# A two-block transformer on one core: round 2 of each feed-forward stage laid out anew, constants multiplied in TensorE's first waits, the first weight piece's rest moved to GpSimd, attention's roundings moved to the end of their slot

## The reference

```python
def swiglu(x, w_in, w_out):
    gate, up = jnp.split(x @ w_in, 2, axis=-1)
    return (jax.nn.silu(gate) * up) @ w_out
...
for l in range(DEPTH):
    mod = cond @ ada_w[l] + ada_b[l]
    shift, scale, gate = jnp.split(mod, 3, axis=-1)
    h = rms_norm(x, norm_g[l]) * (1.0 + scale[:, None, :]) + shift[:, None, :]
...
for i in range(DEPTH):
    h = layer_norm(DN_ALPHA * h + 0.5 * swiglu(h, ffn_w_in[i, 0], ffn_w_out[i, 0]), ln_g[i, 0], ln_b[i, 0])
    ...
    h = layer_norm(DN_ALPHA * h + m, ln_g[i, 1], ln_b[i, 1])
    h = layer_norm(DN_ALPHA * h + 0.5 * swiglu(h, ffn_w_in[i, 1], ffn_w_out[i, 1]), ln_g[i, 2], ln_b[i, 2])
```

## Time and profile before

| | |
|---|---|
| median of 3 runs | 2767.73 us (2767.6 to 2770.81) |
| profiled execution, own time | 2771.28 us |
| its span, first to last instruction | 2769.8 us |
| TensorE busy | 2661.6 us, 96% |
| VectorE busy | 1942.5 us, 70% |
| ScalarE busy | 1068.2 us, 39% |
| GpSimd busy | 574.2 us, 21% |
| granted TensorE clock, mean | 0.987 |

### The profile page before, as it was taken

One profiled execution on the slowest core, in us unless ns is written; L12 is line 12 of the kernel. 1 busy time (PEld: TensorE's weight loads), 2 busy tenths in 40 slices (PEclk: granted clock), 3 DMA queues, 4 the chain that ended last, 5 costly groups with the idle time before them and its releaser, 6 DMA issues.

```text
span 2769.8 us, 38462 instructions
## 1 busy us (share of the span) xinstructions
PE 2661.6 (96%) x15907; PEld 2312.8 (83%) x15907; DVE 1942.5 (70%) x2631; ACT 1068.2 (39%) x1518; POOL 574.2 (21%) x366
## 2 busy tenths in 40 slices
PE   5999999999999999999999999999999999989998
PEld 5777877678899998888899988999978778779997
DVE  5888744456788875548888788888744643888887
ACT  3434555552433434343333333343322222343332
POOL 1112000011344400001444214443000000044430
PEclk9999999999999999999999999999999999999999
DMA  7444221112233332222333323333323223223331
GB/s 263 140 145 132 77 61 61 61 62 76 92 103 111 92 107 77 92 61 63 106 107 97 117 77 102 112 92 107 126 83 107 73 68 103 61 92 107 92 122 46
DMA packets 289857, 268.32 MB, mean 97 GB/s; under 512 B 10567, under 2 KB 256593, under 8 KB 288401
## 3 DMA queue, kind: packets, MB, share of 16 engines
q1 hardware_dynamic: 286448, 256.98, 30.0%
q0 software_dynamic: 2368, 6.64, 0.7%
q10 hardware_dynamic: 864, 2.23, 0.2%
HBM read 263.72 MB, written 2.10 MB: 96 GB/s over the span
## 4 chain that ended last, share of the span: by engine, by line
PE 77%; DVE 15%; ACT 4%; issue 2%; DMA 1%; POOL 1%; SPq 0%; DVEq 0%; ACTq 0%; POOLq 0%
PE psum L351 13%; PE psum L353 13%; PE psum L352 13%; PE psum L429 7%; PE psum L430 6%; PE psum L431 6%; PE psum L408 2%; PE psum L407 2%; PE psum L406 2%; DVE w_lo L336 2%; DVE acc L525 1%; PE psum L3176 1%; DVE stat L674 1%; PE psum L2720 1%; DVE acc L684 1%
## 5 line engine op out<-in xcount | busy, mean ns | idle before, releaser
L351 PE MATMUL psum<-h_hi,w_hi 128*128 128x256 f32 (+1 forms) x2288 | 741.8, 324 | 27.8 <-DVE w_lo L1046 15.4
L353 PE MATMUL psum<-h_hi,w_lo 128*128 128x256 f32 (+1 forms) x2288 | 724.0, 316 | 0.0
L352 PE MATMUL psum<-h_lo,w_hi 128*128 128x256 f32 (+1 forms) x2288 | 723.5, 316 | 0.0
L351 PEld LDWEIGHTS psum<-h_hi,w_hi 128*128 128x128 f32 x2288 | 442.2, 193 | 61.2 <-issue 17.5
L352 PEld LDWEIGHTS psum<-h_lo,w_hi 128*128 128x128 f32 x2288 | 442.4, 193 | 28.5 <-issue 4.8
L353 PEld LDWEIGHTS psum<-h_hi,w_lo 128*128 128x128 f32 x2288 | 441.6, 193 | 27.0
L982 POOL TENSOR_TENSOR val<-w_raw 128x512 f32<-128x512 f32 x72 | 105.8, 1470 | 1285.1 <-DMA w_raw<-in_ffn_w_in 990.1
L336 DVE TENSOR_TENSOR w_lo<-w_raw,w_hi 128x2048 fp32r<-128x2048 f32 x102 | 234.5, 2311 | 146.6 <-ACT w_hi L331 137.8
L525 DVE SCALAR_TENSOR_TENSOR acc<-psum,acc 128x512 f32<-128x512 f32 x416 | 270.5, 680 | 47.6 <-PE psum L431 47.6
L351 PE MATMUL psum<-t_hiffn,w_hi 128*128 128x256 f32 x864 | 247.0, 286 | 2.5 <-DVE f_cffn L1063 2.5
L331 ACT ACTIVATE w_hi<-w_raw 128x2048 fp32r<-128x2048 f32 x104 | 197.2, 1911 | 134.2 <-PE psum L431 69.0
(11 more groups left out here) (429 smaller groups left out, 5396.0 us busy)
## 6 DMA issues: line engine op xcount, KB each, us to landing
w_raw<-in_ffn_w_in SPq DMA_DIRECT2D x176, 512.0 KB, 5.1
w_raw<-in_ffn_w_out SPq DMA_DIRECT2D x88, 512.0 KB, 6.4
w_raw<-in_ret_w_in SPq DMA_DIRECT2D x48, 512.0 KB, 4.7
ada_raw<-in_ada_w SPq DMA_DIRECT2D x32, 512.0 KB, 4.6
w_raw<-in_odd_w_in SPq DMA_DIRECT2D x32, 512.0 KB, 4.9
w_raw<-in_even_w_in SPq DMA_DIRECT2D x24, 512.0 KB, 7.4
w_raw<-in_gla_w_in SPq DMA_DIRECT2D x24, 512.0 KB, 4.8
ada_first<-in_ada_w SPq DMA_DIRECT2D x8, 1024.0 KB, 9.5
```

What stands on the lines that cost most here:

```text
L351: k.nc.tensor.matmul(out, ws, xs, start=first, stop=False)
L352: k.nc.tensor.matmul(out, ws, xl, start=False, stop=False)
L353: return k.nc.tensor.matmul(out, wl, xs, start=False, stop=last)
```

## The change

Five places are edited.

1. Way into the seven products: in `scalar_ffn` and `vector_ffn` the units of piece a of round 2 are rounded during round 1's last steps, T1's rounding goes behind them, and round 2 gets an order of its own (`vector_seventh`) in which A1 of piece b goes ahead of S, and piece o of round 1 is made in halves. TensorE waits for `w_s` separately (at P1), SyncE for `w_s` too before it overwrites that buffer. GpSimd loads the norm rows one sum set later.
2. The start: `tensor_warm` multiplies constants and the first tile of x into a bank that nobody reads, 5, 2 and 3 times.
3. The two parts of `lower` leave the gaps between the first row blocks and go behind them.
4. The first piece's rest is made by GpSimd in four parts (`gpsimd_first`), for which TensorE waits part by part.
5. In attention the piece at point 1 of a slot is rounded at the slot's end, and some additions to `acc` go ahead of a maximum or a piece.

```diff
@@ sync_piece
-    if n >= SLOTS:
+    if n == SLOTS:
+        k.nc.sync.wait_ge(*k.at("pool_w", ("rest", 3)))
+    elif n > SLOTS:
         k.nc.sync.wait_ge(*k.at("w_lo", n - SLOTS))
+        if PIECES[n - SLOTS][1:] == ("b", SEVEN):
+            k.nc.sync.wait_ge(*k.at("w_s", n - SLOTS))
@@ tensor_seven
+        if x == 1 and r == SEVEN:
+            pe.wait_ge(*k.at("w_s", n))
@@ scalar_ffn
+    n = AT[stage, "a", SEVEN]
+    scalar_unit_a22(k, n)
     scalar_hidden_split(k, stage, 1, 0)
     scalar_hidden(k, stage, 1, 1)
+    scalar_unit_s(k, n)
     scalar_hidden_split(k, stage, 1, 1)
+    scalar_unit_a1(k, n)
     scalar_t(k, stage, "T1")
-    n = AT[stage, "a", SEVEN]
-    scalar_unit_a22(k, n)
-    scalar_unit_s(k, n)
-    scalar_unit_a1(k, n)
...
         scalar_first(k, stage, r, 0)
+        scalar_unit_a1(k, AT[stage, "b", r])
         if r == SEVEN:
+            scalar_piece(k, AT[stage, "o", r - 1])
             scalar_unit_s(k, n)
-            scalar_piece(k, AT[stage, "o", r - 1])
-        scalar_unit_a1(k, AT[stage, "b", r])
+            scalar_products(k, stage, r, 0)
+            scalar_first(k, stage, r, 1)
+            scalar_hidden_split(k, stage, r, 0)
+            n = AT[stage, "a", r + 1]
+            scalar_unit_a22(k, n)
+            scalar_products(k, stage, r, 1)
+            scalar_unit_s(k, n)
+            scalar_hidden_split(k, stage, r, 1)
+            scalar_unit_a1(k, n)
...
@@ new, called by vector_ffn for round 2
+def vector_seventh(k, stage):
+    r = SEVEN
+    n, n_o = AT[stage, "b", r], AT[stage, "o", r - 1]
+    vector_unit_a22(k, n)
+    vector_mid(k, stage, r, 0, 0)
+    vector_mid(k, stage, r, 0, 1)
+    vector_unit_a1(k, n)
+    vector_mid(k, stage, r, 0, 2)
+    vector_piece_half(k, n_o, 0)
+    vector_c11(k, stage, r, 0)
+    vector_unit_s(k, n, 0)
+    vector_c12(k, stage, r, 0)
+    vector_unit_s(k, n, 1)
+    vector_products(k, stage, r, 0)
+    k.nc.vector.wait_ge(*k.at("f_h", (stage, r, 0)))
+    vector_mid(k, stage, r, 1, 0)
+    vector_hidden_split(k, stage, r, 0)
+    vector_mid(k, stage, r, 1, 1)
+    vector_piece_half(k, n_o, 1)
+    vector_mid(k, stage, r, 1, 2)
+    n = AT[stage, "a", r + 1]
+    vector_unit_a22(k, n)
+    vector_c11(k, stage, r, 1)
+    vector_c12(k, stage, r, 1)
+    vector_products(k, stage, r, 1)
+    vector_unit_s(k, n, 0)
+    vector_unit_s(k, n, 1)
+    vector_hidden_split(k, stage, r, 1)
...
@@ the start
+def gpsimd_first(k):
+    po, n = k.nc.gpsimd, AT["even", "qf", 0]
+    po.wait_ge(*k.at("w_hi", n))
+    for c in range(4):
+        x = slice(c * T, (c + 1) * T)
+        po.tensor_tensor(k.lo(n)[:, x], k.w_raw[:, buffer(n), x], k.hi(n)[:, x].bitcast(F32), SUB
+                         ).then_inc(*k.up("pool_w", ("rest", c)))
+WARM = (5, 2, 3)
+def tensor_warm(k, n):
+    for _ in range(n):
+        k.nc.tensor.matmul(k.bank[6][:], k.ident, k.acc[:, 0, 0:T], start=True, stop=True)
@@ attention
-    {-2: ("odd", "out", 1), 1: ("odd", "out", 2)}, {-2: ("odd", "out", 3), 1: ("ffn00", "a", 0)})]
+    {-2: ("odd", "out", 1), 1: ("odd", "out", 2)}, {-1: ("odd", "out", 3), 1: ("ffn00", "a", 0)})]
         scalar_turned(k, p, 3)
+        scalar_slot_piece(k, p, 1)
         scalar_slot_piece(k, p, 2)
...
+        if p == 4:
+            vector_outs(k, p, 3)
         vector_max(k, p, 3)
-        vector_outs(k, p, 3)
+        if p != 4:
+            vector_outs(k, p, 3)
         vector_filled(k, p, 0, fill)
         vector_scale(k, p, 3)
+        vector_outs(k, p, 4)
         vector_slot_piece(k, p, -1)
-        vector_outs(k, p, 4)
...
     vector_gated(k, 7)
     vector_gated_rest(k, 7)
+    vector_slot_piece(k, 7, 1)
```

More of the change, by code:

```diff
@@ L325, in scalar_piece @@
     if gated(n):
-        k.nc.scalar.wait_ge(*k.at("gated_even" if PIECES[n][0] == "even" else "gated", n))
+        k.nc.scalar.wait_ge(*k.at("gated_even" if PIECES[n][0] == "even" else "pool_w", n))
     else:
@@ L378, in half_step, with project_half @@
                  kk == 0, kk == KD - 1)
-def project_half(k, S, n, half, banks, steps=range(KD)):
+def project_half(k, S, n, half, banks, steps=range(KD), rests=None):
     for kk in steps:
+        if rests and kk % 2 == 0:
+            k.nc.tensor.wait_ge(*k.at(rests, ("rest", kk // 2)))
         if kk % 2 == 0:
@@ L1191, in vector_hidden_split @@
     vector_split(k, s, k.f_h[:, s, :], (stage, r, s), *ffn_oh(k, stage, r))
+def vector_seventh(k, stage):
[26 more added lines that the diff above has]
+    vector_hidden_split(k, stage, r, 1)
+    vector_outs_ffn(k, stage, r - 1, range(2))
+    vector_unit_a1(k, n)
+    vector_outs_ffn(k, stage, r - 1, range(2, 4))
+    n = AT[stage, "b", r + 1]
+    vector_unit_a22(k, n)
+    vector_unit_s(k, n, 0)
+    vector_outs_ffn(k, stage, r - 1, range(4, 6))
+    vector_unit_s(k, n, 1)
+    vector_outs_ffn(k, stage, r - 1, range(6, 8))
 def vector_ffn(k, stage):
@@ L1214, in vector_ffn @@
     vector_hidden(k, stage, 1, 0)
+    n = AT[stage, "a", SEVEN]
+    vector_unit_a22(k, n)
     vector_hidden_split(k, stage, 1, 0)
     vector_hidden(k, stage, 1, 1)
+    vector_outs_ffn(k, stage, 0, range(2))
+    vector_unit_s(k, n, 0)
+    vector_outs_ffn(k, stage, 0, range(2, 3))
     vector_hidden_split(k, stage, 1, 1)
[L1218 to L1223, removed]
+    vector_outs_ffn(k, stage, 0, range(3, 4))
     vector_unit_s(k, n, 1)
     vector_unit_a1(k, n)
+    vector_t_rest(k, stage, "T1")
     vector_outs_ffn(k, stage, 0, range(4, 8))
-    n = AT[stage, "b", SEVEN]
-    vector_unit_a22(k, n)
-    for r in range(SEVEN, ROUNDS):
+    vector_seventh(k, stage)
+    for r in range(SEVEN + 1, ROUNDS):
         last = r == ROUNDS - 1
         vector_mid(k, stage, r, 0, 0)
-        if r > SEVEN:
-            vector_piece(k, AT[stage, "o", r - 1])
+        vector_piece(k, AT[stage, "o", r - 1])
         vector_mid(k, stage, r, 0, 1)
-        if r == SEVEN:
-            vector_unit_s(k, n, 0)
         vector_mid(k, stage, r, 0, 2)
-        if r == SEVEN:
-            vector_unit_s(k, n, 1)
-            vector_piece(k, AT[stage, "o", r - 1])
         vector_unit_a1(k, AT[stage, "b", r])
@@ L1412, in scalar_start @@
     sc.activation(k.vcol[:], k.bank[0][:, 0:P], ACT.Copy).then_inc(*k.up("vcol", 0))
+    scalar_piece(k, AT["even", "qf", 0])
     sc.wait_ge(*k.at("lb_max", 0))
     sc.activation(k.lbt[:], k.lbt[:], ACT.Exp).then_inc(*k.up("lb_exp", 0))
-    scalar_piece(k, AT["even", "qf", 0])
     sc.wait_ge(*k.at("col8", "even"))
@@ L1465, in vector_start @@
         vector_modulated_tile(k, "even", t)
-    vector_first(k, 3)
-    ve.wait_ge(*k.at("vcol", 0))
-    vector_lower(k)
-    vector_first(k, 4)
-    vector_lower_sum(k)
-    for n in range(5, KD - 1):
+    for n in range(3, KD - 1):
         vector_first(k, n)
@@ L1474, in vector_start @@
     vector_first(k, KD - 1, 1, 2)
-    vector_piece(k, AT["even", "qf", 0])
+    ve.wait_ge(*k.at("vcol", 0))
+    vector_lower(k)
     mod = k.mod[:, 0, 0:16]
@@ L1681, in tensor_even @@
         bk = [flip(i, b) for b in range(8)]
-        pe.wait_ge(*k.at("w_lo", n_qf))
         if i == 0:
             pe.wait_ge(*k.at("mod", (0, "scale")))
-            project_half(k, S, n_qf, 0, (bk[0], bk[1]))
+            project_half(k, S, n_qf, 0, (bk[0], bk[1]), rests="pool_w")
             tensor_turn_tile(k, S, 2, STREAM[S])
@@ L1698, in tensor_even @@
         else:
+            pe.wait_ge(*k.at("w_lo", n_qf))
             pe.wait_ge(*k.at("e_u", i - 1))
@@ L2030, in gpsimd_program @@
     gpsimd_start(k)
+    gpsimd_first(k)
     gpsimd_even(k)
```

25 lines of the change are left out of this document (19 added, 6 removed).

## The result

| | before | changed |
|---|---|---|
| median, 5 runs each | 2767.73 us | 2739.3 us (2738.66 to 2740.87) |
| ratio, 95% interval | | 0.9896 (0.9884 to 0.9907) |
| profiled execution, own time | 2771.28 us | 2738.66 us |
| its span | 2769.8 us | 2737.2 us |

The forecast was 2736.4 us, a gain of 31.3. The medians are 28.4 apart, the two profiled spans 32.6.

What follows compares the result with a forecast made beforehand. TensorE, busy 96%, bounds the kernel, so only its waits or a faster clock can save time. Ways in 20.8, start 5.0 and attention 5.5 sum to 31.3 us: from the 2767.73 median to 2736.4 us, range 2722 to 2751 (own range 2729 to 2743).

Steps and rivals of the forecast that it cites:

- The pause and the clock behind it: Way into each feed-forward stage: waits of 26.7/4 us plus 2.35 us of slow clock, 9.0 us wasted per stage.
- What is late next: Rounds 2 and 3: S of piece b late by 0.5 us at P1; then waits of 1.9 at P4, 1.1 at P5.
- the heavier rival: Rounds 2 and 3: sums of 8 us and more, long pause in round 3, clock falls; 1.8 per stage, 2750 us; chance 0.26.
- Sums beside VectorE: GpSimd's four sums for piece b of round 3 take 7.2 us beside VectorE's work, instead of 5.6 us undisturbed.
- The sum of the stages: Ways into the four feed-forward stages: 9.0 + 0.3 less 1.1 and 3.0, 5.2 us each, 20.8 us in all.
- The start: Kernel start: first product's 48 matmuls end at 45.2, a gain of 5.8, taken as 5.0 us; bounds 1.2 and 6.5.
- GpSimd's four parts: Start, 35.1 to 40.5: run beside VectorE's rests of the features and may make the first 0.5 to 1 us late.
- five multiplications: Start: constants multiplied from 19.4, three slow at 1.8 us and two fast at 0.9, ending at 26.3.
- the first seven multiplications: Start: five before the turning, so it runs at full clock in 3.8 us, and two more after it, to 31.7.
- the 48 matmuls of the first products: Start: after three last constant multiplications they run at full clock in 5.8 us instead of 8.4.
- Attention: Waits in slots 0, 2, 4 and 7 shortened by reordering: sum stated as 6.0, taken as 5.5 us; bounds 3.5 and 6.3.
- Its four terms: Attention: 1.67 us each in slots 0 and 2, some 1.0 in slot 4, 1.33 in slot 7.

Runs made afterwards that it cites:

- the gate in parts: Changed kernel with GpSimd's multiplication of a piece by the gate in four 128x512 instructions in place of one of 128x2048: ratio 0.9886.
- the last kernel: Changed kernel with first piece and gate in parts, two last constant multiplications, S earlier, two additions to acc between products and split: 2724.54 us, ratio 0.9841.

## Why the prediction held, step by step

- **The pause and the clock behind it** (9.0 us a stage wasted): right. The 3.9 us wait and the stretch at 0.80 went in all four stages. That the wait itself lets the clock fall is borne out by moving A1 alone: the wait went, and with it the slow stretch in three stages of four. The 2.35 us of clock per stage were those of one execution; others with the same wait lose less in some stages.
- **What is late next**: right in place and size. P1 of the second half waits 0.55 us (0.5 forecast), P4 of round 3 1.64 (1.9), P5 0.85 (1.1). The cause given, that `w_s` of round 3's piece a stands behind the products, is shown: with S earlier both waits vanish. The forecast also reckoned with no loss of clock at these waits, since they are short. That held in the changed kernel, but the fall behind the 1.73 us wait in ffn10, with A1 moved alone, shows that the heavier rival was nearer than its text says.
- **Sums beside VectorE**: right. GpSimd's four sums for piece b of round 3 ran from 731.08 to 738.20, 7.1 us, where I took 7.2. The full lock of the two engines' port that the Trainium skill states ("SBUF — State Buffer", section "SBUF: two separate sides") shows plainly in attention (4.85 us in place of 0.48). In the ways in, though, it cost no more than the forecast. That this is because the sums are short instructions, between which VectorE gets its turn, is argued; what the gate in parts shows in attention fits it.
- **The sum of the stages**: 20.8 forecast; 21.8 by matched starts, about 20.2 against the mean of three executions with the old ways in, and 20.2 with that place alone.
- **The start**: the term that was too large, 5.0 against 3.1 to 3.5. Two steps of it failed. "GpSimd's four parts ... may make the first 0.5 to 1 late" was 1.9 (1.4 of it at the columns behind `mod`, of which I had not thought), so the first product came at 41.1 and not at 39.4. Part of this is a slip in the sum: five multiplications, three at 1.8 and two at 0.9, end at 26.6 by its own prices, not at 26.3; they ended at 27.19, and the one-column sums at 35.95 instead of 35.3. And the first seven multiplications, with the turning at full clock, won nothing, as the row blocks end at 32.6 or earlier either way; only the last three count. That the sums come earlier is the work of the turning's earlier start and of the row blocks without gaps. That the 48 matmuls of the first products would run in 5.8 us at full clock was right. The half-clock stretch and these products in the changed kernel, beside the earlier trace rows:

```profile
35.87:39.28 3.41, 3.41 (x5) 1.39 (x5) 2.88 (x5) 1.31 (x3) 3.41 (x4) 0.50 0.97 381
41.13:46.95 5.82, 5.82 (x48) 5.82 (x49) 4.77 (x9) 3.84 (x6) 0.00 (x0) 1.00 1.08 368
```

- **Attention**: 5.0 against 5.5. Its four terms (1.67, 1.67, 1.0 and 1.33) add up to 5.7, not to the 6.0 that it states. The slots gave 1.8, 1.8, 1.3 and 1.5. Of these 6.4, 1.1 were lost again at the wait for the probabilities and 0.3 before it. The 1.1 is a step that the prediction lacked: earlier work of VectorE now meets GpSimd's long multiplication by the gate. The trace of the kernel before had such a meeting to see, in a place where TensorE did not wait for it; the same pair takes 0.48 us in its other six places:

```profile
576.63 4.65 DVE L2330 TENSOR_SCALAR o_P<-o_P,o_l 128x128 f32<-128x128 f32 x2
```

- **The last 3 us**: the forecast took a gain worked out from one profiled execution off the median. That execution stood 3.5 us above its median, and the changed kernel's 0.6 below its own, which is the whole difference between the spans (32.6) and the medians (28.4). Much of it is chance in where the clock is at half: 2 us at the start and about 1.6 on the ways in. With 20.2 for the ways in, 3.3 for the start and 5.0 for attention the parts add up to 28.5. Against the forecast of 31.3 that is 1.7 less at the start, 0.6 less on the ways in and 0.5 less in attention. The interval of the ratio is 3.2 us either way, so the agreement of 28.5 with the medians is no proof of these parts.

## What to carry to other kernels

When the worst wait of a chain goes, follow the lists of all engines on to the next one: here each removed wait let a smaller one appear (3.9, then 1.6 at P4, then 1.55 at an output), and three more orders were tried until none of these was left. A piece of work that moves to GpSimd is not free for VectorE: cut it into short instructions, and look at what VectorE does in that time, above all tiny operations on the critical path. Short instructions shorten the delay and don't remove it: at the start GpSimd's work was in four parts, and two operations on 128x8 still took 1.71 us instead of 0.34. An operation that is put ahead of others in order to free something must have its own input by then: read the time at which that is ready before moving it.

## What the runs showed that was not expected

- An operation of VectorE on 128x2 elements takes 2.99 us, and two on 128x128 take 4.85, where GpSimd works on 128x2048; with four instructions of 128x512 in its place the longest takes 1.09. The four take 5.14 us in all instead of 4.58.
- A wait costs TensorE more than its idle time. Matmuls of 256 columns start 0.12 us apart; around the wait at P5 in the changed kernel they stand so:

```profile
746.61 0.28 PE L356 MATMUL psum<-h_lo,w_hi 128*128 128x256 f32 x1
746.73 0.28 PE L357 MATMUL psum<-h_hi,w_lo 128*128 128x256 f32 x1
747.86 0.38 PE L355 MATMUL psum<-h_hi,w_hi 128*128 128x256 f32 x1 [0.85 <-DVE consts L1068]
748.08 0.28 PE L356 MATMUL psum<-h_lo,w_hi 128*128 128x256 f32 x1
748.20 0.28 PE L357 MATMUL psum<-h_hi,w_lo 128*128 128x256 f32 x1
```

From 746.73 to 748.08 are 1.35 us where 0.24 would do: the listed 0.85 us cost 1.11. The 1.64 at P4 cost 1.91 in the same way (743.40 to 745.55). Together that is 3.0 us of the 3.06 a stage that the last kernel, without these waits, won on the changed one, where the list has 2.5.

- Code that nobody touched moves by some microseconds. The four executions with the old start spread over 4.9 us at the same product, the last one before attention. From 30 us up to it, the clock was at half for 20.5 us in the earliest of them (the way in alone) and for 30.4 in the latest (attention alone), and half of this difference is the 4.9. An effect of under 3 us is to be read between the places it touches, not off the whole time.
